# Where and when the first expert weights are loaded in a one-core hybrid decoder step with a mixture of experts

## The reference

```python
def _hier_moe(x, rg_w, rg_b, re_w, re_b, w1, w3, w2):
    pg = softmax(x @ rg_w + rg_b)                 # 4 groups, take the best
    le = (x @ re_w + re_b)                        # 32 experts; 8 in the chosen group
    v2, i2 = top_k(softmax(le in the group), 2)   # two experts for a token
    v2 = v2 / sum(v2)
    y = 0
    for each expert e:                            # w1, w3: 1024x256, w2: 256x1024
        h = silu(x @ w1[e]) * (x @ w3[e])
        y += (gate[:, e] * h) @ w2[e]
    return y
y = x + _hier_moe(rms_norm(x)); out = rms_norm(y)
```

## Time and profile before

| | |
|---|---|
| median of 3 runs | 1462.38 us (1459.76 to 1464.94) |
| time of the profiled execution | 1459.85 us |
| its span | 1458.0 us |
| TensorE matmul busy | 1278.5 us, 88% of the span |
| VectorE busy | 648.4 us, 44% |
| expert stage | from 1062.5 us to the end, some 396 us |
| HBM read | 295.45 MB, written 27.01 MB |

### The profile page before, as it was taken

The page is one execution under the profiler, slowest core; times in us unless marked ns, Lnnn a source line. Parts: engine busy times, 40 slices in busy tenths (PEclk is TensorE's granted clock), DMA queues, the critical chain, the costliest instruction groups (busy, mean ns, idle before and its releaser), DMA issues. The chain is left out here.

```text
span 1458.0 us, 32247 instructions
## 1 busy us (share of the span) xinstructions
PE 1278.5 (88%) x13766; PEld 982.5 (67%) x13766; DVE 648.4 (44%) x1339; ACT 409.0 (28%) x856; POOL 470.0 (32%) x398
## 2 busy tenths in 40 slices
PE   7988899999999999999999989978637999996960
PEld 6877699889879979978988978767533333332320
DVE  2749663444345246246335535445361322211228
ACT  3142134234234224323423422422101222211214
POOL 1615362272264145327236327324001111111100
PEclk9999899999999999999999999989857999998985
DMA  9878438636925834852773562480088999999977
GB/s 272 261 206 252 150 109 260 200 103 206 287 85 174 265 110 154 265 174 90 239 240 103 177 203 90 130 133 19 32 295 292 361 320 379 370 363 371 368 288 309
DMA packets 273911, 317.28 MB, mean 218 GB/s; under 512 B 15196, under 2 KB 253352, under 8 KB 272336
## 3 DMA queue, kind: packets, MB, share of 16 engines
q1 hardware_dynamic: 261352, 277.51, 60.7%
q10 hardware_dynamic: 5792, 20.78, 4.1%
q0 software_dynamic: 6624, 16.92, 3.0%
HBM read 295.45 MB, written 27.01 MB: 221 GB/s over the span
## 5 line engine op out<-in xcount | busy, mean ns | idle before, releaser
L1533 PE MATMUL psum<-arena 128*128 128x256 f32 (+3 forms) x1536 | 310.2, 356 | 2.7 <-issue 2.7
L1533 PEld LDWEIGHTS psum<-arena 128*128 128x128 f32 x1536 | 257.4, 194 | 32.8 <-issue 3.4
L2378 PE MATMUL psum<-arena 128*64 128x512 f32 (+1 forms) x832 | 171.2, 627 | 21.2 <-DMA arena<-in_exp_w 21.2
L1236 DVE COPY_PREDICATED arena<-arena,psum 128x128 f32<-128x128 int32 x280 | 85.3, 305 | 141.0 <-PE psum L1722 134.1
L1529 PE MATMUL psum<-arena 128*128 128x128 f32 x1152 | 137.6, 279 | 3.6 <-DVE arena L1102 3.6
L1529 PEld LDWEIGHTS psum<-arena 128*128 128x128 f32 x1152 | 133.1, 195 | 6.2 <-issue 5.8
L669 POOL TENSOR_TENSOR arena<-arena 128x768 f32<-128x768 f32 (+1 forms) x32 | 59.1, 1846 | 240.6 <-ACT arena L900 240.6
L2378 PEld LDWEIGHTS psum<-arena 128*64 128x64 f32 (+1 forms) x832 | 53.7, 136 | 121.7 <-issue 119.6
L1491 PE MATMUL psum<-arena 64*64 64x64 f32 x3264 | 115.9, 222 | 4.6 <-issue 2.0
L1491 PEld LDWEIGHTS psum<-arena 64*64 64x64 f32 x3264 | 104.0, 136 | 21.5 <-issue 14.1
L1801 PE MATMUL psum<-arena 128*128 128x256 f32 x512 | 117.4, 389 | 0.8 <-ACT arena L977 0.8
(11 more groups left out here) (399 smaller groups left out, 1952.6 us busy)
## 6 DMA issues: line engine op xcount, KB each, us to landing
arena<-in_w_in SPq DMA_DIRECT2D x96, 1024.0 KB, 6.1
arena<-in_exp_w SPq DMA_DIRECT2D x96, 1024.0 KB, 13.1
arena<-in_w_out SPq DMA_DIRECT2D x32, 1024.0 KB, 5.8
arena<-in_w_in SPq DMA_DIRECT2D x24, 512.0 KB, 5.4
arena<-y_d SPq DMA_DIRECT2D x8, 1024.0 KB, 11.9
arena<-in_x_prompt ACTq DMA_DIRECT2D x15, 512.0 KB, 6.0
arena<-in_w_in SPq DMA_DIRECT2D x8, 576.0 KB, 4.9
arena<-in_w_in SPq DMA_DIRECT2D x8, 560.0 KB, 4.3
```

The source lines that it names most:

```text
L1236: ins = v.copy_predicated(h3(att_b)[:, h:h + 2, :], b3(q_mask[4 * half + j], 2, 64), new)
L1533: ins = mm(b[:, 0:n], hT[:, c, :], w[:, c, 0:n], start=(c == 0), stop=(c == KC - 1))
L2378: ins = mm(bank[2 + q % 2][at:at + width, :], xT[q % 2][:, c, at:at + width], w13[n % NB][:, c, :], start=(c == 0), stop=(c == KC - 1))
```

## The change

One of the 32 expert loads is moved into the trunk's last tile, the weight buffers get new places, and two loads get a new place in SP's order.

1. *Expert 0 (the first with a fixed number) is loaded in the trunk.* Its w13 goes over the trunk tiles x, hT, tok and the first val, its w2 over gt, gtm and gti. SP issues the three DMAs behind the conv rows of tile 7, after it has waited for the last readers and writers of these tiles (`s_tail`, `linT_mm`, `kdg`, `atd`, `gc_late`). They stand ahead of the stores of the final states. The trunk's end waits for them (`lead_in`). TensorE no longer waits for expert 0 in the expert stage, and the counts for the other users of buffer 0 are one load lower.
2. *Layout.* The seven w13 parts, the seven w2 parts and the two X buffers, before in one block, are taken one by one so that those of buffer 0 fall on the place above. `borrow`, the routing's scratch, takes from w13 and w2 of buffer 6 as before.
3. *Experts 4 and 5* are issued as soon as `by_rank` is there; before, SP waited for the first two gathers (`xg_in0`, `xg_in1`) first. Now expert 6 is the first behind the gathers.

```diff
@@ in build
+        lead13 = mark + 11 * D
+        lead2 = lead13 + KC * 512 + 14 * D
+        lead = arena[:, lead13:lead13 + KC * 512], arena[:, lead2:lead2 + 2 * D]
@@ in trunk, SP
+            sp.wait_ge(step("s_tail"), 32)
+            done(sp, "linT_mm", NT - 1)
+            done(sp, "kdg", NT - 1)
+            done(sp, "atd", NT - 1)
+            sp.wait_ge(step("gc_late"), 1)
+            w13, w2 = lead[0].rearrange("p (c n) -> p c n", c=KC), lead[1].rearrange("p (c n) -> p c n", c=2)
+            sp.dma_start(w13[:, :, 0:256], A["exp_w1"][0, 0].rearrange("(p c) n -> p c n", c=KC)).then_inc(step("lead_in"), 16)
+            sp.dma_start(w13[:, :, 256:512], A["exp_w3"][0, 0].rearrange("(p c) n -> p c n", c=KC)).then_inc(step("lead_in"), 16)
+            sp.dma_start(w2, A["exp_w2"][0, 0].rearrange("(c p) n -> p c n", c=2)).then_inc(step("lead_in"), 16)
             done(sp, "s_lin", NT - 1)
...
             sp.wait_ge(step("raw_out"), 16)
+            sp.wait_ge(step("lead_in"), 48)
@@ in experts, layout
-    W = KC * 512 + 2 * D
-    wall = take(NB * W)
...
-    X = [take(D) for _ in range(NX)]
+    W13, W2 = KC * 512, 2 * D
+    flat, w2_flat, X = [lead[0]], [lead[1]], []
+    flat += [take(W13) for _ in range(2)]
+    w2_flat.append(take(W2))
+    X.append(take(D))
+    assert take(W13).offset == lead[0].offset
+    flat += [take(W13) for _ in range(3)]
+    w2_flat.append(take(W2))
+    assert take(W2).offset == lead[1].offset
+    flat.append(take(W13))
+    w2_flat += [take(W2) for _ in range(4)]
+    X.append(take(D))
...
@@ in experts, SP
-            for e in range(AT_ONCE):
+            for e in range(1, AT_ONCE):
                 load_w(sp, e, e)
...
+            sp.wait_ge(step("by_rank"), 1)
+            for n in range(AT_ONCE, NB - 1):
+                load_ranked(sp, n)
             for u in range(2):
                 sp.wait_ge(step(f"xg_in{u}"), 16)
-            sp.wait_ge(step("by_rank"), 1)
-            for n in range(AT_ONCE, N_EXP):
+            for n in range(NB - 1, N_EXP):
                 load_ranked(sp, n)
@@ in experts, TensorE, mm1 (and likewise mm2)
                 for at, width, n in QUADS[q]:
-                    pe.wait_ge(w13_in(n % NB), 32 * (n // NB + 1))
+                    if n:
+                        pe.wait_ge(w13_in(n % NB), 32 * (n // NB + (n % NB > 0)))
```

More of the change, by code:

```diff
@@ L219, in build, with trunk @@
         mark = used[0]
+        lead13 = mark + 11 * D
+        lead2 = lead13 + KC * 512 + 14 * D
+        lead = arena[:, lead13:lead13 + KC * 512], arena[:, lead2:lead2 + 2 * D]
         with stage_semaphores(nc) as stage:
-            trunk(nc, stage, A, O, lambda a, b: arena[:, a:b], take, psum, bank, const, masks, x2_d, h2_d, lg, rows_d, so_d)
+            trunk(nc, stage, A, O, lambda a, b: arena[:, a:b], take, psum, bank, const, masks, x2_d, h2_d, lg, rows_d, so_d, lead)
         used[0] = mark
         with stage_semaphores(nc) as stage:
-            experts(nc, stage, A, O, arena, take, bank, const, masks_f, x2_d, h2_d, lg, y2_d)
-def trunk(nc, ctx, A, O, arena_cols, take, psum, bank, const, masks, x2_d, h2_d, lg, rows_d, so_d):
+            experts(nc, stage, A, O, arena, take, bank, const, masks_f, x2_d, h2_d, lg, y2_d, lead)
+def trunk(nc, ctx, A, O, arena_cols, take, psum, bank, const, masks, x2_d, h2_d, lg, rows_d, so_d, lead):
     ident = const[:, C_ID:C_ID + P]
@@ L320, in region @@
         return arena_cols(a, b)
+    for held, first, last in ((lead[0], x, val[0]), (lead[1], gt, gti)):
+        a, b = held.offset % 53200, held.offset % 53200 + held.shape[-1]
+        assert a >= first.offset % 53200 and b <= last.offset % 53200 + last.shape[-1]
     def within(first, last, start, n):
@@ L1878, in _, with experts @@
             route(NT - 1)
-def experts(nc, ctx, A, O, arena, take, bank, const, masks_f, x2_d, h2_d, lg_flat, y2_d):
+def experts(nc, ctx, A, O, arena, take, bank, const, masks_f, x2_d, h2_d, lg_flat, y2_d, lead):
     ident = const[:, C_ID:C_ID + P]
@@ L1906, in experts @@
     NX = 2
-    W = KC * 512 + 2 * D
-    wall = take(NB * W)
-    assert NB == 7
-    w13 = [wall[:, b * W:b * W + KC * 512].rearrange("p (c n) -> p c n", c=KC) for b in range(NB)]
-    w2 = [wall[:, b * W + KC * 512:b * W + W].rearrange("p (c n) -> p c n", c=2) for b in range(NB)]
-    X = [take(D) for _ in range(NX)]
+    W13, W2 = KC * 512, 2 * D
[10 more added lines that the diff above has]
+    X.append(take(D))
+    assert NB == len(flat) == len(w2_flat) == 7
+    w13 = [ap.rearrange("p (c n) -> p c n", c=KC) for ap in flat]
+    w2 = [ap.rearrange("p (c n) -> p c n", c=2) for ap in w2_flat]
     xT_flat = [take(D) for _ in range(2)]
@@ L1926, in experts @@
     fs, eps = take(4 * NTT), take(1)
-    spare = [0]
+    spare = [0, 0]
     def borrow(n):
-        spare[0] += n
-        assert spare[0] <= W
-        return wall[:, 6 * W + spare[0] - n:6 * W + spare[0]]
+        b = 0 if spare[0] + n <= W13 else 1
+        spare[b] += n
+        assert spare[1] <= W2
+        return (flat[6], w2_flat[6])[b][:, spare[b] - n:spare[b]]
     slot_hot = borrow(T2 * P)
@@ L1958, in experts @@
     x2 = [w2[(N_EXP - NB + t // 2) % NB][:, t % 2, :] for t in range(NT)] + [w2[1][:, 0, :]]
-    flat = [w13[b].rearrange("p c n -> p (c n)") for b in range(NB)]
     y2 = [flat[t // 2][:, 2048 * (t % 2):2048 * (t % 2) + 2048] for t in range(NTT)]
@@ L2392, in mm2 @@
                 for at, width, n in QUADS[q]:
-                    pe.wait_ge(w2_in(n % NB), 16 * (n // NB + 1))
+                    if n:
+                        pe.wait_ge(w2_in(n % NB), 16 * (n // NB + (n % NB > 0)))
                 for b in range(2):
```

## The result

Over 20 runs of each kernel, 1468.76 us median after (1464.55 to 1475.94) against 1463.22 before: the ratio is 1.0035, 95% interval 1.0024 to 1.0046, or 5.1 us slower (3.5 to 6.7). The ratio leaves out one run of the kernel before that took 1930.88 us, and is not just the quotient of the two medians, which lie 5.5 us apart. The profiled execution of after has a span of 1470.2 us, 12.2 more than before. That number is not the effect: 5.6 us of it are there by 959.78 us, before any changed instruction, most of them in the first 100 us. So the two traces are compared stage by stage, from a mark in each. These are two lines of the page after.

What follows compares the result with a forecast made beforehand. It took buffers freed at TensorE's pace, hanging on mm1(0) and the first gathers, as the bound. Terms 0 + 0 + 3.2 (first gather) + 0 = +3.2 us on the 1462.38 median gave 1465.6, range 1458 to 1471.

Steps and rivals of the forecast that it cites:

- +3.2 forecast: Whole kernel: sum of all terms, +3.2 us, all of it from the first gather landing later.
- What bounds the kernel: Expert stage: SP's loads wait for buffers freed at TensorE's pace, so time follows mm1(0) and the first gathers.
- Rival A: Queue from 1064 to 1395 us is the bound throughout; one load less saves 8.5 us, time 1453.9; chance 0.12.
- The first gather: Behind the barrier: beside expert 5's load it lands after 7.7 us instead of 4.5, +3.2 us; bounds 0 and 8.3.
- A full half share: First gather taking turns with the weight queue: +1.4 us; part of a rival from 0 to 1.4, chance 0.14.
- Shorter fixed loads and the layout at 0: Expert stage: fixed loads ending 8.7 us earlier gain 0, as nobody waits for them; new buffer places cost 0.
- Cost of adding: 0, hidden behind the last tile: Trunk's last tile: expert 0's loads, in by 1016 us at the latest, delay nothing; 0 us.
- nothing is pushed away: Trunk, 1000 to 1009 us: only 15 GB/s moves there, so expert 0's loads displace no other transfers.
- The lower bound is 0 too: Expert 0's load in the trunk: no gain either, since nobody in the trunk waits less; 0 us.
- rival C: Both first gathers stand behind the weights until expert 5 is through: +5 to +8.3 us, 1467.4 to 1470.7; chance 0.17.

Runs made afterwards that it cites:

- twice the traffic: Kernel before plus six 1 MB memory-to-memory transfers in the last tile, nothing written into the arena; ratio 1.0024 against before, 3.5 us slower.
- both: Changed kernel with expert 0 loaded behind the state stores and experts 4 and 5 behind the first two gathers; ratio 0.9994 against before.
- one ahead: Changed kernel with expert 0 loaded behind the state stores and only expert 4 ahead of the gathers; ratio 1.0003 against before.
- pairs with expert 0 late: Changed kernel with expert 0 behind the state stores, experts 4 and 5 behind the gathers, w13 then w2 issued for two experts together; ratio 0.9976 against before.
- loads in pairs: Kernel before, but from expert 7 on SP issues w13 of two experts, then their two w2; ratio 0.9962, 5.6 us faster than before.
- 4 and 5 behind: Changed kernel with experts 4 and 5 again waiting for the first two gathers, expert 0 still in the trunk; ratio 1.0016 against before.
- traffic only: Kernel before plus three 1 MB memory-to-memory transfers where the changed kernel loads expert 0, nothing written into the arena; ratio 1.0023 against before.

## Why the prediction was right, and where not

The time measured against before, +5.1 us, is above the +3.2 forecast and inside the range; the median after, 1468.76, is 3.2 us above the 1465.6 given. At 0.35% it lies a little above the 0.3% that I had set as the bound, so it counts as slower, which had 0.27, and not as the same, which had 0.59.

**What bounds the kernel: right.** mm1(0) was later by 2.7 us from the barrier, and the whole stage by 2.96. SP waited for mm2 three times as before, longer, and for mm1 ahead of expert 7. The kernels that change how early weights come but not when the gather lands keep the stage at 395.4 to 396.0; the two that hold up the gather have 398.4 and 399.4. Only the profile with twice the traffic has 397.7 with an undisturbed gather (4.61 us), so a single stage length is good to some 2 us, and the landing of the gather and the start of mm1(0) carry the argument. Rival A, worth 8.5 us, failed in each kernel that gave it room (the changed one, both, one ahead, pairs with expert 0 late); loads in pairs then showed what had held it.

**The first gather: right.** 7.31 us to landing for 7.7 forecast, so 2.8 and not 3.2. A full half share would have made 1.4; in the second kernel with this collision the gather took 8.22.

**Shorter fixed loads and the layout at 0: right** within the interval of the kernel with both causes removed (0.9994, 0.9971 to 1.0017).

**The load in the trunk, "Cost of adding: 0, hidden behind the last tile": this step failed.** The load went out at 1005.31, which on before's clock is 999.7, between the 998 and 1007 worked out. But I had asked only who is queued behind it, and whose stores. I said "nothing is pushed away" because the stretch moved 15 GB/s. Two of the transfers in that stretch (1000 to 1009 us) were instruction packets, 33 KB of some 135. TensorE stalled 1.9 us in mid-tile and then ran on a lower clock; the middle part grew by 4.1 us. The state stores, forecast at 1029, were at 1032.7 on that clock. "The lower bound is 0 too" closed the range on the side where the surprise lay.

How the +5.1 divides in ordinary runs stays open. The two causes together account for it, since without both the time is back (0.9994). The gather's 2.8 to 3.0 us leave some 2 for the stall, and the runs with the stall alone give 2.3 (4 and 5 behind), 3.4 (traffic only) and 3.5 us (twice the traffic, the only one clear of zero). But the kernel with the gather's collision alone was 5.4 us slower (2.3 to 8.5), as much as the changed one, with a gather of 8.22.

That the result lies where rival C has its times (1467.4 to 1470.7) is a coincidence: C needs a gather of over 9 us, and that did not happen. The range held because it was made wide for C, and not because the trunk's cost was foreseen.

## What to carry to other kernels

Before moving a load earlier, find what ends the wait of the queue that it leads: here it was a buffer freed by TensorE, and changing which of two waits stands first in the queue gave 5.6 us where an earlier start gave nothing. An empty stretch of the DMA engines is not free to fill: look for small transfers that something waits for, such as a gather on the path or, as these runs suggest, the instruction queue in a part with very many short matmuls. Keep a bulk load that nobody needs soon out of both.

## What the runs showed of the hardware

Traffic of 3 MB beside a part with 64x64 matmuls made TensorE stall 1.9 to 3.8 us without any named releaser, also where the transfers wrote nothing into the arena. In all five stalls, with those of the 6 MB, the wait ended 2.6 to 2.9 us after a late packet of the instruction queue. The same 3 MB beside the output projection (128x256 matmuls) left the profile without such a stall; there the packets of that queue came 30 us apart (1021.0 and 1051.5). A gather of 128 rows landed after 4.3 to 4.6 us with no weight load beside it and after 7.3 and 8.2 with one. The granted clock fell behind the stall in three of four kernels (0.60 to 0.77 over the next 6 us) and stayed at 1.00 in one. The granted clock of the very same instructions differs between runs (1.00, or 0.65 to 0.67, around 990 to 1000 us), and the last tile without a stall by up to 5 us (102.0 to 107.3), with at most 16 GB/s of transfers beside it; single profiles are best compared over short parts between two fixed instructions.
